# Order of work in three places of a hybrid decoder trunk: attention's tail, the gated inputs of the recurrence, and the scaled rows of the gelu half

## The reference

```python
gate, xb = split(rms_norm(x) @ w_in)           # 1408 columns each
gate = gelu(gate);  xb = causal_depthwise_conv(xb)     # width 4
r, i = sigmoid(xb @ gate_r + b_r), sigmoid(xb @ gate_i + b_i)   # 16 blocks
log_a = -8 * r * softplus(-lambda)
h_t = exp(log_a) * h_(t-1) + sqrt(1 - exp(2*log_a)) * (i * xb)
x = x + (gate * h) @ w_out
```

## Time and profile before

| | us |
|---|---|
| median of three runs | 1377.47 |
| the profiled execution: time | 1379.55 |
| the profiled execution: span | 1377.7 |
| TensorE busy | 1324.7 (96% of the span) |
| VectorE busy | 795.8 (58%) |
| ScalarE busy | 642.3 (47%) |
| GpSimd busy | 10.5 (1%) |
| mean granted TensorE clock | 0.985 of full speed |

### The profile page before, as it was taken

One profiled execution on the slowest core, in us unless ns is written; L12 is line 12 of the kernel. 1 busy time (PEld: TensorE's weight loads), 2 busy tenths in 40 slices (PEclk: granted clock), 3 DMA queues, 4 the chain that ended last, 5 costly groups with the idle time before them and its releaser, 6 DMA issues.

```text
span 1377.7 us, 18659 instructions
## 1 busy us (share of the span) xinstructions
PE 1324.7 (96%) x7469; PEld 1003.3 (73%) x7469; DVE 795.8 (58%) x818; ACT 642.3 (47%) x593; POOL 10.5 (1%) x12
## 2 busy tenths in 40 slices
PE   6999999999997999999999999999999999999996
PEld 6988999999997888885357885346887345888433
DVE  4995565655589759991029981008984105996101
ACT  5466444343379547750037771007773005874100
POOL 0000000000011000000000000000000000000000
PEclk9999999999999989999999999999999999999999
DMA  9331555455454689999999999999999999999995
GB/s 306 116 123 31 154 172 167 140 191 172 129 165 153 228 316 363 369 363 341 409 411 412 411 408 394 399 407 409 413 410 406 379 408 411 412 407 412 412 406 235
DMA packets 149574, 426.13 MB, mean 309 GB/s; under 512 B 7665, under 2 KB 65649, under 8 KB 135153
## 3 DMA queue, kind: packets, MB, share of 16 engines
q1 hardware_dynamic: 149488, 424.90, 81.5%
HBM read 423.82 MB, written 1.05 MB: 308 GB/s over the span
## 4 chain that ended last, share of the span: by engine, by line
PE 83%; DMA 7%; DVE 4%; ACT 3%; issue 2%; SPq 1%; DVEq 0%; ACTq 0%
PE P L1633 60%; PE P L2041 12%; DMA over_gates_raw<-in_moe_w_gate 5%; PE P L2065 3%; PE P L1928 2%; DMA raw<-in_moe_w_down 1%; PE P L1949 1%; SPq L587 1%; PE P L1983 1%; ACT whi L651 1%; PE P L1743 1%; DVE raw_lo L1049 1%; DVE xc L1314 1%; DMA raw<-in_w_in_even 1%; PE P L1664 1%
## 5 line engine op out<-in xcount | busy, mean ns | idle before, releaser
L1633 PE MATMUL P<-hn_hi,whi 128*128 128x272 f32 (+1 forms) x640 | 187.9, 294 | 14.5 <-DVE hn_lo L1350 8.5
L1388 DVE TENSOR_TENSOR raw_lo<-raw,whi 128x2048 fp32r<-128x2048 f32 x84 | 189.5, 2285 | 12.3 <-ACT whi L903 11.8
L903 ACT ACTIVATE whi<-raw 128x2048 fp32r<-128x2048 f32 x84 | 161.0, 1918 | 56.2 <-PE P L1633 40.4
L1633 PE MATMUL P<-whi,xe_hi 128*128 128x512 f32 x448 | 179.9, 402 | 7.1 <-DVE over_gates_lo L1388 7.1
L1633 PE MATMUL P<-hn_hi,raw_lo 128*128 128x272 f32 (+1 forms) x640 | 186.1, 291 | 0.0
L1633 PE MATMUL P<-hn_lo,whi 128*128 128x272 f32 (+1 forms) x640 | 185.4, 290 | 0.0
L1049 DVE TENSOR_TENSOR raw_lo<-raw,whi 128x2048 fp32r<-128x2048 f32 (+3 forms) x72 | 150.9, 2117 | 47.5 <-ACT whi L651 47.4
L1633 PE MATMUL P<-whi,xe_lo 128*128 128x512 f32 x448 | 178.1, 398 | 0.0
L1388 DVE TENSOR_TENSOR over_gates_lo<-over_gates_raw,whi 128x2048 fp32r<-128x2048 f32 x72 | 162.9, 2286 | 19.3 <-ACT whi L903 19.0
L903 ACT ACTIVATE whi<-over_gates_raw 128x2048 fp32r<-128x2048 f32 x72 | 137.3, 1916 | 42.4 <-PE P L1633 19.1
L1608 DVE TENSOR_TENSOR hb<-silu,P 128x512 f32<-128x512 f32 (+1 forms) x16 | 9.9, 622 | 220.7 <-PE P L2041 220.7
(11 more groups left out here) (293 smaller groups left out, 2065.3 us busy)
## 6 DMA issues: line engine op xcount, KB each, us to landing
raw<-in_moe_w_up SPq DMA_DIRECT2D x64, 1024.0 KB, 15.9
raw<-in_moe_w_gate SPq DMA_DIRECT2D x64, 1024.0 KB, 14.9
over_gates_raw<-in_moe_w_down SPq DMA_DIRECT2D x64, 1024.0 KB, 16.8
over_gates_raw<-in_moe_w_gate SPq DMA_DIRECT2D x48, 1024.0 KB, 18.8
raw<-in_moe_w_down SPq DMA_DIRECT2D x40, 1024.0 KB, 15.4
over_gates_raw<-in_moe_w_up SPq DMA_DIRECT2D x32, 1024.0 KB, 15.0
over_xb_raw<-in_moe_w_up SPq DMA_DIRECT2D x16, 1024.0 KB, 16.2
raw<-in_w_in_even SPq DMA_DIRECT2D x10, 1024.0 KB, 10.5
```

The costliest lines, as they stand in the source:

```text
L903: act.activation(whi[u % HI][:, :], moe_raw[k % MOE_RAW][:, :], ACT.Copy).then_inc(hi_ready, 1)
L1388: dve.tensor_tensor(moe_lo(k), moe_raw[k % MOE_RAW][:, :], whi[u % HI][:, :].bitcast(F32), ALU.subtract).then_inc(lo_ready, 1)
L1633: last = pe.matmul(dst, lhs, rhs, start=start and n == 0, stop=stop and n == 2)
```

## The change

- VectorE makes the gated input (`gated_input(j)`, six products, at units `U_BAND + 4` to `U_GELU + 3`, each ahead of that unit's split), GpSimd's six products go.
- VectorE makes the gelu half's rows earlier: group 0 at unit `U_BAND + 4`, group 1 at `U_BAND + 5`, groups 2 and 3 at `U_GELU`, all ahead of that unit's split.
- TensorE's first gelu unit waits for the groups one by one as its first column of tiles reaches them.
- ScalarE takes `gates(3)` to `gates(5)` behind the splits of gelu units 0 to 2, no longer ahead of them.
- Attention: pairs 2 and 3 put their output into banks 2 and 3, which the scores have left, and `values(2)` and `values(3)` wait for the masked scores (long there) in place of `attn_low`. `values(0)` moves ahead of the LayerNorm's mean. On ScalarE the four `high` copies move behind the high halves of the swish rows, `weights(2)` moves behind the LayerNorm's scaled rows; on VectorE `log_weights(3)` moves ahead of all swish rows and the four `attn_low` behind the low halves of the rows.
- The halved LayerNorm parameters (one small VectorE instruction) are made behind the first norm's low halves, not ahead of the first split.

```diff
@@ values_bank
-            return 6 + p % 2
+            return (6, 7, 2, 3)[p]
@@ block.gpsimd
-            for j, ms in enumerate(BAND_UNITS):
-                m0, n = ms[0], len(ms)
-                pool.wait_ge(xb_ready, TAPS * KL)
-                pool.wait_ge(gates_ready, j + 1)
-                pool.tensor_tensor(ig[:, m0:m0 + n], ig[:, m0:m0 + n], xc[:, m0:m0 + n], ALU.mult).then_inc(xi_ready, 1)
@@ scalar: attention
                 inverse_root(rs[:, 0], P[:, 1, 0:T], CONV_CH, var_root)
-                weights(2)
                 act.preload_act_table_set("exp_and_others")
...
-                high(0)
+                weights(2)
                 for c in range(CT):
                     act.wait_ge(ln_out, c + 1)
                     act.activation(scr[:, c], uin[:, c], ACT.Tanh).then_inc(ln_tanh, 1)
-                high(1)
                 weights(3)
                 for c in range(CT):
                     act.wait_ge(ln_silu, c + 1)
                     act.activation(mix_hi[:, c], uin[:, c], ACT.Copy).then_inc(ln_hi, 1)
+                high(0)
+                high(1)
                 high(2)
                 high(3)
@@ scalar: main loop
-                if U_BAND <= u - GATES_AHEAD < U_GELU:
+                if U_BAND <= u - GATES_AHEAD and u < U_GELU:
                     gates(u - GATES_AHEAD - U_BAND)
...
                     split_hi(u)
+                if U_GELU <= u < U_GELU + GATES_AHEAD:
+                    gates(u - GATES_AHEAD - U_BAND)
@@ vector: attention
-                attn_low(0)
-                for c in range(2):
+                log_weights(3)
+                for c in range(CT):
                     silu_row(c)
-                log_weights(3)
-                for c in range(2, CT):
-                    silu_row(c)
-                attn_low(1)
                 for c in range(CT):
                     dve.wait_ge(ln_hi, c + 1)
                     dve.tensor_tensor(mix_lo[:, c], uin[:, c], mix_hi[:, c].bitcast(F32), ALU.subtract).then_inc(ln_lo, 1)
-                attn_low(2)
-                attn_low(3)
+                for p in range(HEADS // 2):
+                    attn_low(p)
@@ vector: new
+            def gated_input(j):
+                m = slice(BAND_UNITS[j][0], BAND_UNITS[j][-1] + 1)
+                dve.wait_ge(xb_ready, TAPS * KL)
+                dve.wait_ge(gates_ready, j + 1)
+                dve.tensor_tensor(ig[:, m], ig[:, m], xc[:, m], ALU.mult).then_inc(xi_ready, 1)
@@ vector: main loop
-            dve.tensor_scalar(half_ln[:, :], v("ln_g", 0, 2 * CT), 0.5, None, ALU.mult).then_inc(half_ready, 1)
             split_lo(0)
             norm_low(0)
+            dve.tensor_scalar(half_ln[:, :], v("ln_g", 0, 2 * CT), 0.5, None, ALU.mult).then_inc(half_ready, 1)
             for u in range(U_MOE):
-                if u == U_GELU:
+                if U_BAND + 4 <= u < U_GELU + 4:
+                    gated_input(u - U_BAND - 4)
+                if u == U_BAND + 4:
                     dve.wait_ge(unit_used, U_BAND)
                     dve.wait_ge(xb_ready, TAPS * KL)
-                    for c in range(2):
-                        normed_rows(c)
-                elif u in (U_GELU + 1, U_GELU + 2):
-                    normed_rows(u - U_GELU + 1)
+                    normed_rows(0)
+                elif u == U_BAND + 5:
+                    normed_rows(1)
+                elif u == U_GELU:
+                    normed_rows(2)
+                    normed_rows(3)
@@ tensor: features
+                        if scaled and m == 0 and kk % 2 == 0:
+                            pe.wait_ge(rows_normed, kk // 2 + 1)
@@ tensor: values
                 elif p >= 2:
-                    pe.wait_ge(attn_lo, p - 1)
+                    pe.wait_ge(zm_ready, HEADS // 2)
@@ tensor: attention
             taps(U_DIAG + 1)
+            values(0)
             conv_mean()
             later(2)
             conv_variance()
-            values(0)
             values(1)
@@ tensor: gelu half
-                if n == 0:
-                    pe.wait_ge(rows_normed, KD // 2)
-                features(u, hn_hi, hn_lo, gelu_bank(n), cols=slice(META, T))
+                features(u, hn_hi, hn_lo, gelu_bank(n), cols=slice(META, T), scaled=n == 0)
```

More of the change, by code:

```diff
@@ L1636, in features @@
             def features(u, x_hi, x_lo, bank, k0=0, start=True, stop=True, cols=slice(0, T), norm=None, sums=None,
-                         mixed=False):
+                         mixed=False, scaled=False):
                 k, w = UNITS[u][2], UNITS[u][3]
```

## The result

The changed kernel took 1369.42 us (median of 6 runs, 1367.91 to 1371.92) against 1378.5 us of the kernel before on the same chip; ratio 0.9939, 95% interval 0.9925 to 0.9953, which is a gain of 8.4 us with 6.5 to 10.3 as interval; the two medians alone lie 9.1 us apart. A second timing gave 0.9929 (0.9912 to 0.9946). The forecast was 8.8 us and 1368.7 us. The profiled execution took 1370.34 us with a span of 1368.5 us, 9.2 less than the one before.

What follows compares the result with a forecast made beforehand. TensorE, busy 96% of the span, was taken as the bound, with idle ahead of the output projection and the gelu half. Savings of 5.9 + 1.5 + 1.4 = 8.8 us give 1368.7 us, range 1366.3 to 1372.5.

Steps and rivals of the forecast that it cites:

- VectorE's queue (5.9 us): Ahead of the gelu half: VectorE's reordered work lets TensorE start at 419.5, not 425.38, saving 5.9 us.
- GpSimd's stretching: Ahead of the gelu half: GpSimd's products stretch VectorE's instructions beside them through a shared port, by 3.1 us.
- slower: Rival (3%): stretched prices are VectorE's own, so VectorE bounds the gelu half's start; 5.0 us slower, 1382.5.
- The clock (1.5 us): Gelu half's start: with idle cut to 2.6 us the clock no longer falls to half speed, saving 1.5 us.
- the forecast's own sign: Ahead of the gelu half: the forecast is wrong if the clock shows half after 418.
- this 10%: Rival (10%): the clock falls all the same ahead of the gelu half; 7.3 us saved, 1370.2.
- The rest of the odd layer ("some 5 stay"): Output projection's third unit: of TensorE's 10 us margin towards VectorE's side 5.3 go, some 5 stay.
- Attention (1.4 us): Attention's tail: the last `values` starts at 129.75 instead of 131.16, the projection 1.4 us earlier.
- The loads: First expert: weight loads still wait for TensorE, so the whole shift reaches the end; rival (8%): only 3.5 us.
- The sum: Whole kernel: queue 5.9, clock 1.5 and attention 1.4 give 8.8 us, median 1368.7.

Runs made afterwards that it cites:

- pool_products: The changed kernel with the six gated-input products back on GpSimd; ratio to the kernel before 0.9959.
- late_rows: The changed kernel with the gelu half's rows back at the first three gelu units; ratio to the kernel before 0.9960.
- band_only: The changed kernel with attention's part of the change undone; ratio to the kernel before 0.9946.
- split_first: The changed kernel with VectorE's first gelu split ahead of row groups 2 and 3; ratio to the kernel before 0.9928.
- split_again: split_first once more, beside the changed kernel on the same chip; ratio to the kernel before 0.9931.
- gelu_first: split_first with each gelu on ScalarE issued ahead of the previous group's high halves of rows (`y_high`); ratio to the kernel before 0.9952.
- values_late: gelu_first with `values(0)` and `values(1)` both behind `later(3)`; ratio to the kernel before 0.9944.
- two_splits: gelu_first with two, not four, high halves of the first expert's weights ahead of the router's work on ScalarE; ratio to the kernel before 0.9911.
- attn_only: The kernel before with attention's part of the change alone; ratio to the kernel before 0.9975.

## Why the prediction was right, and where it was not

- **VectorE's queue (5.9 us).** Right, 6.11 measured. A product took 0.72 with 0.63 start to start (0.65 taken), a group of rows 2.0 to 2.1; the gelu split starts 0.1 us after the band's end (0.2 in the sum), and it is what TensorE waits for. pool_products and late_rows show that both halves of it are needed: with the products on GpSimd 2.6 us of the gain go, and with the rows in their old place 2.4.
- **GpSimd's stretching.** Right as mechanism: casts and scalings are free throughout, and the stretching is back as soon as GpSimd has the products. The rival "slower" is out with it.
- **The clock (1.5 us).** Wrong, and by the forecast's own sign. The step that failed is "The clock fell 5 us after the last band matmul (416.9 to 421.9), so I take it that it no longer falls". In the three executions of the changed kernel it fell 2.3, 2.6 and 3.5 us after that matmul, in pool_products 2.4; in band_only, with the same 2.5 us of idle, it did not. The forecast had given this 10%. The five executions with 0.4 us of idle and no further wait in the first gelu column kept the full clock there (split_first, split_again, gelu_first, values_late, two_splits). The price itself was right: with full clock and no late gelu the stretch to the trunk's end takes 62.15 us, 1.4 to 1.5 less than the changed kernel's 63.6 to 63.7. The Trainium skill, "TensorE: Matmul & The Clock Gate", section "What's actually happening", says that the gate's timing is not tied to the kernel and the turning point varies; the traces agree, with 2.3 to 5.2 us after the last matmul.
- **The rest of the odd layer ("some 5 stay").** Right in the outcome, wrong in the margin. The forecast looked at VectorE's low halves, where 6.2 us were left in the profile, and missed the fourth gelu, where 0.85 were. So even with the clock at full speed about half of its 1.5 us would not have come through: band_only, where it stayed full, gained 0.7 to 0.8. split_first shows the same wait larger, 2.59 us.
- **Attention (1.4 us).** Right, 1.37 to within 0.01 in every kernel with that part unchanged. One slip in its working, 2.54/2 = 1.24 for 1.27, is too small to matter. The forecast had the last `values` start at 129.75; it starts at 128.95 with all before the tail 0.80 earlier, which is the same.
- **The loads.** Right for this change: in the profiled pair, what was gained up to the first expert is still there at the end (8.4 us there, 9.2 at the end). They are the next bound, as gelu_first shows, through ScalarE's queue.
- **The sum.** The stages give 7.5 us, the two timings 8.4 and 9.8 us, with 6.5 to 10.3 and 7.4 to 12.1 as intervals. Both 7.5 and the forecast's 8.8 lie inside them, but 1.5 of the 8.8 was for a cause that did not act, so part of the closeness of 8.8 to the measured times is luck. What makes up the rest is open. Three stretches that the change hardly touches differ between executions. Before attention the taps end at 112.2 to 112.7 us in the five profiles with 3.4 us of half clock there, and at 113.0 to 114.1 in the eight with 6.8. The router had 13.7 us of half clock in both profiles without the band's part (before, attn_only), and 6.8 to 10.2 in eight of the nine that have it and do not delay the router; 3.4 us less is worth 1.6 us of time. If that is an effect of the change, it fills the gap, but so few profiles don't show it. The experts take 866 to 870.5 us to the end, and that does not follow the length of half clock in them (band_only 17.1 us of half clock and 866.4, split_first 12.6 and 868.8).

## What to carry to other kernels

When a wait is removed, look up every wait of the following stretch with its margin, not only the one on the engine that was late: here the bound went from the rows to the split, from there to a gelu behind an unrelated wait in its queue (0.9 us of margin, then 2.6 us of wait), and from there to a weight split ahead of the router (3.4 us of wait). A small idle place of TensorE may cost more than its length, since the clock can fall in it: here up to 1.5 us on top of 2.5. Work on GpSimd is not free for a late VectorE: here making the products itself cost VectorE 0.63 us each, and leaving them to GpSimd 1.1 to 1.2 for each that met one of its instructions.

## What the runs showed of the hardware

The granted clock fell at an idle place of 2.5 us in three executions of the changed kernel and not in band_only, which has the same place; in the 8.6 us place it fell 5.2 and 4.9 us after the last matmul (before, attn_only). In pool_products' 5.1 us it fell after 2.4 us, and in late_rows inside the wait of 3.84 us. Attention's tail, with TensorE busy in short pieces, was hit once in thirteen profiles (band_only) and took 1.25 us more; with the half speed behind it that fall cost 2.8 us. One program's executions spread over 1.1 us (two_splits, four runs) to 9.0 us (late_rows, ten runs), and the profiles show different places of half clock in each. Only before attention is a part of the spread seen to go with the clock: there the taps end 0.4 to 1.9 us later with 6.8 us of half clock than with 3.4.
